# Differential attention on one core: the value product in three rounded single passes instead of one four-byte float32 product

## What is computed

```python
logits = einsum("bqhcd,bkhcd->bhcqk", qb, k) * scale + bias      # c = 2 sets per head, causal
p = softmax(logits, axis=-1)
attn = p[:, :, 0] - lam * p[:, :, 1]
o = einsum("bhqk,bkhe->bqhe", attn, v)                           # 128 values per head
o = rms_norm(o, subln_w, eps=1e-5) * (1.0 - lambda_init)
```

## Time and profile before

| | |
|---|---|
| median of three runs | 2521.91 us |
| the profiled execution, its own time | 2523.18 us |
| its span, first to last instruction | 2521.2 us |
| TensorE busy | 2506.2 us, 99% of the span |
| chain that ended last | TensorE 98%, VectorE 1%, ScalarE 1% |
| VectorE busy | 1822.3 us, 72% |
| ScalarE busy | 1247.9 us, 49% |
| granted TensorE clock | 1.000 over the whole span |
| DMA | 188 GB/s, 61% of the engines' time |

### The profile page before, as it was taken

One profiled execution on the slowest core, in us unless ns is written; L12 is line 12 of the kernel. 1 busy time (PEld: TensorE's weight loads), 2 busy tenths in 40 slices (PEclk: granted clock), 3 DMA queues, 4 the chain that ended last, 5 costly groups with the idle time before them and its releaser, 6 DMA issues.

```text
span 2521.2 us, 42149 instructions
## 1 busy us (share of the span) xinstructions
PE 2506.2 (99%) x15444; PEld 2238.8 (89%) x15444; DVE 1822.3 (72%) x2572; ACT 1247.9 (49%) x1631; POOL 155.6 (6%) x271
## 2 busy tenths in 40 slices
PE   8999999999999999999999999999999999999999
PEld 8999999999898888888888998998898888888887
DVE  6977877787876675766667876778866667576667
ACT  7555555554654444444444754455644444444444
POOL 2222112211100000000000000000000000000000
PEclk9999999999999999999999999999999999999999
DMA  7666556656566566666656555555566656666664
GB/s 216 212 199 199 175 184 192 206 166 196 172 190 193 183 197 189 191 191 190 192 183 198 194 176 176 179 173 168 184 189 188 192 183 198 190 191 192 190 192 151
DMA packets 267240, 474.10 MB, mean 188 GB/s; under 512 B 16673, under 2 KB 50066, under 8 KB 265618
## 3 DMA queue, kind: packets, MB, share of 16 engines
q1 hardware_dynamic: 264194, 457.53, 59.2%
q0 software_dynamic: 2624, 15.00, 1.7%
q10 hardware_dynamic: 336, 0.41, 0.0%
HBM read 470.70 MB, written 2.19 MB: 188 GB/s over the span
## 4 chain that ended last, share of the span: by engine, by line
PE 98%; DVE 1%; ACT 1%; DMA 0%; issue 0%; SPq 0%; ACTq 0%; DVEq 0%
PE ps L1615 23%; PE ps L1616 23%; PE ps L1617 23%; PE ps L1644 16%; PE ps L1646 9%; PE ps L1873 1%; PE ps L1751 0%; PE ps L1971 0%; DMA h<-x 0%; PE ps L1878 0%; PE ps L1810 0%; PE ps L1779 0%; PE ps L2001 0%; PE ps L1729 0%; PE ps L1735 0%
## 5 line engine op out<-in xcount | busy, mean ns | idle before, releaser
L993 DVE TENSOR_TENSOR whl<-raw,whl 128x1024 fp32r<-128x1024 f32 x856 | 1062.5, 1242 | 592.1 <-ACT whl L664 579.5
L664 ACT ACTIVATE whl<-raw 128x1024 fp32r<-128x1024 f32 x856 | 906.7, 1059 | 1086.8 <-PE ps L1617 735.9
L1644 PE MATMUL ps<-xhl,whl 128*128 128x512 f32 x1792 | 623.0, 391 | 0.0
L1646 PE MATMUL ps<-xhl,whl 128*128 128x256 f32 x1792 | 505.4, 282 | 0.0
L1615 PE MATMUL ps<-whl,bhl 128*128 128x512 f32 x1284 | 500.8, 390 | 0.0
L1616 PE MATMUL ps<-whl,bhl 128*128 128x512 f32 x1284 | 499.5, 389 | 0.0
L1617 PE MATMUL ps<-whl,bhl 128*128 128x512 f32 x1284 | 499.5, 389 | 0.0
L1615 PE MATMUL ps<-xhl,whl 128*128 128x256 f32 x1748 | 493.9, 283 | 0.0
L1616 PE MATMUL ps<-xhl,whl 128*128 128x256 f32 x1748 | 488.5, 279 | 0.0
L1617 PE MATMUL ps<-xhl,whl 128*128 128x256 f32 x1748 | 487.9, 279 | 0.0
L1644 PEld LDWEIGHTS ps<-xhl,whl 128*128 128x128 f32 x1792 | 336.4, 188 | 70.9
(11 more groups left out here) (268 smaller groups left out, 2084.6 us busy)
## 6 DMA issues: line engine op xcount, KB each, us to landing
raw<-mlp_w SPq DMA_DIRECT2D x512, 512.0 KB, 4.2
raw<-a_in_proj SPq DMA_DIRECT2D x161, 512.0 KB, 4.5
raw<-a_out_proj SPq DMA_DIRECT2D x64, 512.0 KB, 4.0
raw<-b_w_q SPq DMA_DIRECT2D x32, 512.0 KB, 4.0
raw<-w_k SPq DMA_DIRECT2D x32, 512.0 KB, 4.0
raw<-w_v SPq DMA_DIRECT2D x32, 512.0 KB, 3.6
raw<-b_out_proj SPq DMA_DIRECT2D x32, 512.0 KB, 3.7
cumb<-cum_scratch POOLq DMA_DIRECT2D x8, 1024.0 KB, 7.7
```

Of the source, the lines that this page charges most:

```text
L664: sc.activation(slot_of(s, lo)[0], raw_of(s), ACT.Copy).then_inc(hi_ready, 1)
L993: ve.tensor_tensor(out=low, in0=raw_of(s), in1=hi.bitcast(F32), op=ALU.subtract).then_inc(lo_ready, 1)
L1644: te.matmul(ps[:, f, :].rearrange("p (q n) -> p q n", q=2), wh[:, j, c], xboth[:, :, k, :], start=k == 0, stop=False, skip_group_check=True)
L1646: last = te.matmul(ps[:, f, 0:S], wl[:, j, c], xhi[:, k, :], start=False, stop=k == KT - 1, skip_group_check=True)
```

## The change

`v` and the turned weights are each kept as two float32r halves, and the value product is made with `three`: 9 float32r matmuls of 128 columns for each head in place of 3 float32 matmuls.

- ScalarE writes `vh` and `ath` (the same copies as before, in the rounded type) and counts `v_hi`, `at_hi`. VectorE then makes `vl` in step v7 and `atl` in the `turn_weights` steps, from the same PSUM banks, and counts `v_copied`, `at_copied`.
- The wait for `v_copied` moves from step q0 to step q1.
- `vh` and `vl` lie in a room that shares its addresses with `postw`. So GpSimd's load of the round 2 weights moves from before the attention stage to behind it: it waits until the last head's `ob` has been written (`o_ready`).

```diff
-        postw = sb("postw", [P, D])
+        first_use = ExitStack()
+        postw = sb("postw", [P, D], F32, first_use)
+        first_use.close()
+        v_room = sb("v_room", [P, D], F32R)
...
-        v = mb("v", [P, MT, BLK])
+        vh, vl = (v_room[:, i * MT * BLK:(i + 1) * MT * BLK].rearrange("p (t n) -> p t n", t=MT) for i in range(2))
...
-        att_t = mb("att_t", [P, S + P])
+        ath, atl = mb("ath", [P, S + P], F32R), mb("atl", [P, S + P], F32R)
...
# GpSimd
             zero_y(1)
-            next_postw(2, w["norm_post_mix"][1])
...
                 tab_load(t + 1)
+            pool.wait_ge(o_ready, MT * HG * QG)
+            next_postw(2, w["norm_post_mix"][1])
             next_postw(3, w["norm_post_mlp"][1])
...
# ScalarE
-                        sc.activation(att_t[:, :], ps[:, plan.weights_bank, 0:S + P], ACT.Copy).then_inc(at_copied, 1)
+                        sc.activation(ath[:, :], ps[:, plan.weights_bank, 0:S + P], ACT.Copy).then_inc(at_hi, 1)
...
-                        last = sc.activation(v[:, t, :], ps[:, 5 + t, :], ACT.Copy, scale=rsh[:, t:t + 1])
-                    last.then_inc(v_copied, 1)
+                        last = sc.activation(vh[:, t, :], ps[:, 5 + t, :], ACT.Copy, scale=rsh[:, t:t + 1])
+                    last.then_inc(v_hi, 1)
...
# VectorE
+                    if j == plan.turn_weights[i]:
+                        dve.wait_ge(at_hi, n + 1)
+                        ve.tensor_tensor(out=atl[:, :], in0=ps[:, plan.weights_bank, 0:S + P], in1=ath[:, :].bitcast(F32),
+                                         op=ALU.subtract).then_inc(at_copied, 1)
...
+                if (unit, i) == ("v", 7):
+                    dve.wait_ge(v_hi, g + 1)
+                    for t in range(MT):
+                        last = ve.scalar_tensor_tensor(out=vl[:, t, :], in0=ps[:, 5 + t, :], scalar=rsh[:, t:t + 1],
+                                                       in1=vh[:, t, :].bitcast(F32), op0=ALU.mult, op1=ALU.subtract)
+                    last.then_inc(v_copied, 1)
...
# TensorE
-                        te.matmul(ps[:, plan.out_bank, P:2 * P], att_t[:, 0:P], v[:, 0, i * P:(i + 1) * P], start=True, stop=False,
-                                  skip_group_check=True)
-                        te.matmul(ps[:, plan.out_bank, P:2 * P], att_t[:, P:2 * P], v[:, 1, i * P:(i + 1) * P], start=False, stop=True,
-                                  skip_group_check=True)
-                        te.matmul(ps[:, plan.out_bank, 0:P], att_t[:, 2 * P:], v[:, 0, i * P:(i + 1) * P], start=True, stop=True,
-                                  skip_group_check=True).then_inc(o_done, 1)
+                        dims = slice(i * P, (i + 1) * P)
+                        for c in range(MT):
+                            keys = slice(c * P, (c + 1) * P)
+                            three(ps[:, plan.out_bank, P:2 * P], (ath[:, keys], atl[:, keys]), (vh[:, c, dims], vl[:, c, dims]),
+                                  start=c == 0, stop=c == 1)
+                        three(ps[:, plan.out_bank, 0:P], (ath[:, 2 * P:], atl[:, 2 * P:]), (vh[:, 0, dims], vl[:, 0, dims]),
+                              start=True, stop=True).then_inc(o_done, 1)
...
-                    if (unit, i) == ("q", 0):
-                        pe.wait_ge(v_copied, g)
+                    if (unit, i) == ("q", 1):
+                        pe.wait_ge(v_copied, g)
+                    if (unit, i) == ("q", 0):
```

More of the change, by code:

```diff
@@ L411, in build @@
         q_copied, k_copied, v_copied = sem("q_copied"), sem("k_copied"), sem("v_copied")
+        v_hi, at_hi = sem("v_hi"), sem("at_hi")
         lg_done, lg_ready, ex_ready, at_ready, at_t, at_copied = (
```

## The result

The changed kernel takes 2527.56 us (median of 11 runs, 2527.39 to 2529.38) against 2521.87 us (11 runs, 2521.73 to 2522.53): 5.7 us more, ratio 1.0023 with a 95% interval of 1.0015 to 1.0031. Forecast were 2527.7 us.

A forecast was written before the change was run, and what follows sets the result against it. TensorE, busy 2506.2 of 2521.2 us, was taken to bound the kernel. Terms +5.7 - 0.7 + 0.8 = +5.8 us, added to the 2521.91 us median, gave 2527.7 us; range 2524.2 to 2530.6, the forecast's own 2526.6 to 2528.8.

The forecast's parts named there:

- nine passes for six: TensorE's value product: nine float32r passes at 0.114 us replace 0.67 us a head, +5.7 us over 16 heads.
- wait for `v` in q0: TensorE's only wait of the attention stage, before L1971 in the second group, goes: -0.7 us, at worst 0.
- VectorE, last group: VectorE's new work makes TensorE wait at `ob` transposes, value products and output slabs of j = 9 to 14: +0.8 us.
- VectorE, elsewhere: First three groups: VectorE, busy 257.08 of the stage's 340 us, is idle often enough, so no cost.
- load of `postw`: GpSimd's load, moved behind the last `ob`, lands over 7 us before its first read: no cost.
- quick-load: Value product: a float32r load is quick, 0.064 us a pass, leaving +0.4 us, 2522.4 us; chance 0.12.
- middle-pace rivals: Value product: load-and-matmul pairs of 128 columns take some 0.08 us, giving +2.2 us, 2524.1 us; chance 0.04.
- many-passes rival: Value product: short float32r products run in as many passes as float32, +1.34 us a head, 2542.6 us; chance 0.06.
- what I named as the next in line: `v_copied`, counted by VectorE and asked for at the end of q1, is next late; ready at 1485.9, needed at 1486.5.
- the fit by 0.6 us: At the end of q1, `v_copied` is ready 0.6 us before TensorE asks for it.
- The prediction's own sign of being wrong: A pace of the new passes under 0.1 us or above 0.12, or a TensorE wait in an earlier group.
- The spill rival: VectorE's lateness makes TensorE wait in every group, 3 x 0.8 = +2.4 us, 2530.1 us; chance 0.08.

The follow-up runs named there:

- no low halves made: Changed kernel with nine float32r passes a head, all on high halves, low halves of `v` and the turned weights not made: 2526.24 us.
- The two runs with 64 columns: Changed kernel with six of a head's nine passes narrowed: to 64 moving columns, 2527.73 us; to 64 stationary columns, 2524.47 us.
- the wide passes: Changed kernel with the two products sharing a stationary high half put into one 256-column matmul, three wide and three narrow passes a head: 2524.48 us.

## Why the prediction was right, and where its terms were off

The time was hit within 0.2 us, but that is in part luck. One term was 0.5 us too large and one 0.8 us too small, and what was left over between them was taken back by 0.3 us that the changed kernel gains outside its span, of which the prediction knew nothing (last paragraph of this section). The direction and TensorE's mechanism were right on their own.

| term | forecast | measured, stage | from |
|---|---|---|---|
| nine passes for six | +5.7 | +5.2 | no low halves made |
| wait for `v` in q0 | -0.7 | -0.8 | wait moved alone |
| VectorE, last group | +0.8 | +0.85 | loads beside those of no low halves |
| VectorE, elsewhere | 0 | +0.8 | the same |
| load of `postw` | 0 | +0.1 | load moved alone |

**The passes.** The mechanism was right: the load of 128 stationary columns sets the pace of passes that move 64 or 128 columns. The two runs with 64 columns show it from both sides, and the wide passes a third time. What was off is the size. I took 0.114 us between 0.110 and 0.117; the float32r passes of 128 columns take the 0.111 us that the earlier trace rows had shown. The 0.116 us of the 256-column stream belongs to that stream and is no property of the format. From a head's first load to the transposes' there are 1.03 us, just the 1.026 that I had added up, but with a late first transpose in it (0.14), and 0.05 us come back in the loads behind; that effect my sum did not have at all.

**The Trainium skill against the rows.** By the Trainium skill ("TensorE: Matmul & The Clock Gate", section "LDWEIGHTS (loading the stationary operand)") the estimate was +4.7 us for this term, by the rows +5.7; measured are +5.2, right between. The rule itself, that a load goes with its number of columns, agrees with the runs as far as they reach: 0.111 us for 128, and at most 0.06 for 64. The fast load of the Trainium skill (same page, section "Weight-path perf modes — Fast Weight Load (FWL) and DoubleRow"), which it has for types that are not float32, does not show in float32r: the load of `ath` lasts 192 ns (median) in the changed kernel and is paced as a float32 one. With this, the quick-load and the middle-pace rivals fall. The many-passes rival falls too: a short float32r product is one pass of 0.111 us.

**The wait for `v`.** Right, and so was what I named as the next in line in the second group: `v_copied` is in time for q1 there.

**VectorE in the last group.** Right in place, order and size (`ob`, then `atl`, then the output slab: idle for 0.48, 0.27 and 0.31 us; what TensorE loses by them is 1.65 - 0.80 = 0.85, against the run without low halves). But the sum leading there was lucky. I counted a subtraction with 0.56 us; queued among others it delays the next instruction by 0.47 only. In exchange, the 1.3 us of idle time could not all be used: 0.55 us of it is still idle in the changed kernel, before the split at 1741.51.

**VectorE elsewhere, the step that failed.** "In the first three groups VectorE is idle often enough", and the fit by 0.6 us taken for all of them. The prediction's own sign of being wrong, a wait in an earlier group, came. The mean over the stage was no evidence on single steps. In the second group TensorE waited 0.3 us for `ob` and 0.3 for `atl`, and at the third slab of output block 0 0.4 us for the low half of `v`; the three set TensorE back by 0.8 us in all. The fit that I worked out held for groups that are followed by q slabs; after the second group an output block follows, and I gave its wait no working. As for `ob`: the lateness that 1.4 us of new work makes in v7 is not absorbed in VectorE's next pause. The logits behind it come later, so ScalarE's exponentials do, so does ScalarE's next split, and VectorE then idles for that. ScalarE waited 13.2 us for `nmax`, which VectorE makes from the logits, in the changed kernel, against this line of the kernel before (8.1 us with the wait for `v` moved, and in both runs without the low half of `v`):

```profile
ACT lg L931 <- DVE nmax L1536: 7.5, 7, 2.5
```

The run without the low half of `v` has none of TensorE's waits, so none of them comes without it; the one for `atl` takes both new works, for the run with the low half of `v` alone has no such line. The path through ScalarE is read from the timelines and was not tested by itself. The spill rival (in every group, +2.4) is thus partly true, in the second group and in output block 0 only.

The medians differ from before by 0.1 to 0.6 us less than the stages do in most of these kernels, and most of that lies outside the span. An execution's time is longer than its span from first to last instruction: by 1.96 us (median) in the kernel before and as much without low halves, by 1.77 with the low half of `v` alone, and by 1.61 to 1.64 in every kernel whose VectorE makes `atl`. So the changed kernel gains 0.3 us there that no engine's stage shows. What in it is shorter stays open.

## What to carry to other kernels

A matmul that moves fewer columns than its weight load takes to load costs the load. Splitting one float32 product (two recorded passes of 0.111 us) into three single passes of 128 columns is therefore a loss of half. Whether the same split pays at 256 columns and more no run here tries. What saves time at this size is fewer or narrower loads, such as moving both halves side by side behind one load. And when an engine that works ahead is given more to do, ask at each place where the critical engine waits for it, not for its mean load; a work's lateness can travel over a third engine.

## What the runs showed of the hardware

- A float32r pass of 128 x 128 costs 0.111 us with 128 moving columns and the same with 64; with 64 stationary and 128 moving columns 0.06, which either side may set; with 128 stationary and 256 moving columns 0.116 to 0.117. Widths between 128 and 256 moving columns were not measured.
- Behind the last float32r load of a product the first load of a float32 transpose comes after 0.14 us, and the three transposes' loads then take 0.31 instead of 0.36 us in all. A head's nine passes thus cost 0.32 us more than six, a little less than three times 0.111.
- Two new works on VectorE cost 0 and 0.6 us alone and 1.4 together (medians), above the run without either. My reading is that each uses up slack that would have hidden the other.
